# A weight stream through places in SBUF: norms in place, Z as a ring place, one single-use place more, and loads in another order

## The reference

```python
def first_block(x, ...):
    for layer in range(2):
        m = conv_mixer(x, ...) if layer % 2 == 0 else rglru_mixer(x, ...)
        x = layer_norm(ALPHA * x + m, ln1_g[layer], ln1_b[layer])
        f = moe(x, w_router, b_router, moe_w1[layer], moe_w3[layer], moe_w2[layer])
        x = layer_norm(ALPHA * x + f, ln2_g[layer], ln2_b[layer])
    return x

def moe(...):                      # 16 experts, the best 2 of one group of 4 for each token
    ...
    hb = jax.nn.silu(xb @ w1[e]) * (xb @ w3[e])      # w1, w3, w2: 1024 x 1024 each, fp32
    return hb @ w2[e]

def rglru_mixer(...):
    u = x @ w_in;  y, xr = split(u);  xr = causal_depthwise_conv(xr, c_dw) + c_dw_b
    r = sigmoid(heads(xr) @ w_gate_a + b_gate_a);  i = sigmoid(heads(xr) @ w_gate_x + b_gate_x)
    log_a = -8 * r * softplus(-lam);  a = exp(log_a)
    h = associative_scan(a, sqrt(1 - a * a) * (i * xr))     # h[t] = a[t] h[t-1] + b[t]
    return (gelu(y) * h) @ w_out
```

## Time and profile before

| | us |
|---|---|
| runs (3) | 1814.17, 1814.87, 1815.21 |
| median | 1814.87 |
| profiled execution, its own device time | 1813.63 |
| span of the profiled execution | 1812.1 |
| PE busy in the span | 1719.1 (95%) |
| DVE busy | 798.0 (44%) |
| ACT busy | 618.4 (34%) |
| the DMA queue q1 (SP's) | 541.10 MB, 74.5% of 16 engines' span |

### The profile page before, as it was taken

How to read it: one execution, slowest core, us unless ns; L and a number is a source line. 1 busy time by engine, 2 the same in 40 slices (tenths; PEclk the granted TensorE clock), 3 DMA queues, 4 the chain that set the end, 5 groups by cost and what they waited for, 6 DMA issues and landing times.

```text
span 1812.1 us, 23943 instructions
## 1 busy us (share of the span) xinstructions
PE 1719.1 (95%) x9988; PEld 1111.4 (61%) x9988; DVE 798.0 (44%) x1538; ACT 618.4 (34%) x1179; POOL 121.2 (7%) x143
## 2 busy tenths in 40 slices
...
GB/s 390 204 218 418 422 423 422 422 424 420 420 420 418 242 173 422 424 422 423 422 423 422 419 420 420 221 138 140 166 184 186 186 163 163 120 125 186 186 185 25
DMA packets 75810, 544.88 MB, mean 301 GB/s; under 512 B 8496, under 2 KB 8496, under 8 KB 10032
## 3 DMA queue, kind: packets, MB, share of 16 engines
q1 hardware_dynamic: 75024, 541.10, 74.5%
...
## 4 chain that ended last, share of the span: by engine, by line
PE 65%; DMA 23%; DVE 7%; ACT 3%; issue 1%; POOL 1%; SPq 1%; DVEq 0%; ACTq 0%
PE PS L1076 21%; DMA ring<-in_w 13%; PE PS L350 12%; PE PS L352 11%; PE PS L351 11%; DMA F<-in_w 6%; PE PS L1053 2%; DMA ring<-in_a_w_in 2%; PE PS L1088 2%; DVE wl L333 2%; DMA ring<-in_odd_w_in 2%; PE PS L789 1%; ACT wh L327 1%; PE PS L554 1%; SPq L315 1%
## 5 line engine op out<-in xcount | busy, mean ns | idle before, releaser
L1076 PE MATMUL PS<-ring,F 128*64 128x512 f32 x2112 | 477.0, 597 | 38.7 <-DMA ring<-in_w 33.6
L333 DVE TENSOR_TENSOR wl<-ring,wh 128x512 fp32r<-128x512 f32 x512 | 368.3, 738 | 170.3 <-ACT wh L327 167.8
L327 ACT ACTIVATE wh<-ring 128x512 fp32r<-128x512 f32 x512 | 319.5, 631 | 271.7 <-PE PS L352 266.0
L1076 PEld LDWEIGHTS PS<-ring,F 128*64 128x64 f32 x2112 | 143.6, 136 | 354.7 <-issue 258.7
L350 PE MATMUL PS<-xh,wl 128*128 128x256 f32 x1168 | 336.6, 288 | 2.4 <-DVE wl L333 2.3
L351 PE MATMUL PS<-xl,wh 128*128 128x256 f32 x1168 | 330.4, 283 | 0.0
L352 PE MATMUL PS<-xh,wh 128*128 128x256 f32 x1168 | 330.3, 283 | 0.0
L350 PEld LDWEIGHTS PS<-xh,wl 128*128 128x128 f32 x1168 | 223.8, 192 | 5.7 <-DVE wl L333 2.7
L351 PEld LDWEIGHTS PS<-xl,wh 128*128 128x128 f32 x1168 | 223.9, 192 | 0.6
L352 PEld LDWEIGHTS PS<-xh,wh 128*128 128x128 f32 x1168 | 223.9, 192 | 0.0
L350 PE MATMUL PS<-wh,xl 128*128 128x512 f32 x352 | 142.5, 405 | 6.9 <-DVE xl L467 3.4
...
## 6 DMA issues: line engine op xcount, KB each, us to landing
ring<-in_w SPq DMA_DIRECT2D x264, 1024.0 KB, 26.4
F<-in_w SPq DMA_DIRECT2D x60, 1024.0 KB, 26.2
ring<-in_ffn_up SPq DMA_DIRECT2D x44, 1024.0 KB, 4.9
early<-in_w SPq DMA_DIRECT2D x40, 1024.0 KB, 26.4
ring<-in_ffn_down SPq DMA_DIRECT2D x22, 1024.0 KB, 4.9
Z<-in_w SPq DMA_DIRECT2D x10, 1024.0 KB, 25.9
XT<-in_w SPq DMA_DIRECT2D x10, 1024.0 KB, 25.1
ring<-in_even_w_in SPq DMA_DIRECT2D x9, 1024.0 KB, 19.6
```

Source lines behind the costliest of these rows:

```text
L327: act.e.activation(self.wh[:, p % NPIECE, :], self.piece_source(p), ACT.Copy).then_inc(*self.up("w_hi", p))
L333: dve.e.tensor_tensor(self.wl[:, p % NPIECE, :], self.piece_source(p), f32(self.wh[:, p % NPIECE, :]), ALU.subtract).then_inc(*self.up("w_ ...
L1076: t = pe.e.matmul(PS[64 * half:64 * half + 64, bank, :], lhs(k), weights[:, a:a + 512], start=(k == 0), stop=(k == 7))
```

## The change

- **Norms behind mixers in place.** `vector_residual` writes ALPHA * x + m back to X; the norm and the transposes then work on X. Behind `moe0` the norm goes from PSUM to X as well, behind `moe1` it still goes to Z. The new function `norm_buffer` says which. The code for overflowing experts keeps its saved values in F in place of Z (it isn't executed with these inputs).
- **Z a ring place.** Up to `aq0` Z is a thirteenth ring place, for dense chunks too.
- **One single place more.** Slot 23 is F[2304:4352]. Only the fourth chunk of a MoE (w1 of expert 0, last quarter) uses it, and LOAD_ORDER moves that chunk's load back, from fourth to eighteenth of its MoE. So 24 chunks can be in SBUF when a MoE begins, in place of 23.
- **Loads in the order in which places come free.** FIRST_SLOTS has a new order. In layer 0 eleven ring loads come ahead of the F places. In layer 1 the F places 16, 15, 14 and 13 stand between ring loads, each for itself.
- **The recurrences' buffers by head.** xc, Tt, ig and R of one head lie together (2048 columns), which is slot 16 for head 0, 15 for head 1, 14 for head 2 and 13 for head 3; each of these waits only for its head's `od_join`. The buffers gq and odd_gh, odd_gl move to F[12672:14720].
- **The two row DMAs** leave ACT. SP issues them behind the third `aq0` chunk (`sync_rows`).

```diff
-RING, SMALL_RING, EXTRA = 12, 7, 11
+RING, SMALL_RING, EXTRA = 12, 7, 12
...
-F_SLOTS, SPLIT_SLOTS, Z_SLOT, XT_SLOT = range(12, 17), range(17, 21), 21, 22
-FIRST_SLOTS = ([12, 13] + [None] * 8 + [14, 15, 16] + [None] * 4 + [17, 18, 19, 20, 21, 22],
-               [None] * 8 + [12, 13, 14, 15, 16] + [None] * 4 + [17, 18, 19, 20, 21, 22])
+F_SLOTS, SPLIT_SLOTS, Z_SLOT, XT_SLOT, ONCE_SLOT = range(12, 17), range(17, 21), 21, 22, 23
+FIRST_SLOTS = ([12, 13] + [None] * 11 + [14, 15, 16, None, ONCE_SLOT, None, 17, 18, 19, 20, XT_SLOT],
+               [None] * 8 + [16, 15, None, None, 14, None, 13, None, 12, ONCE_SLOT, None, 17, 18, 19, 20, XT_SLOT])
+LOAD_ORDER = list(range(len(KIND)))
 
 
 def _place_stream():
+    for layer in range(2):
+        m, at = CHUNK[f"moe{layer}"], FIRST_SLOTS[layer].index(ONCE_SLOT)
+        LOAD_ORDER[m + 3:m + at + 1] = LOAD_ORDER[m + 4:m + at + 1] + [m + 3]
     last, loads = [None] * (RING + EXTRA), [0] * (RING + EXTRA)
-    for n, kind in enumerate(KIND):
-        slots = list(range(RING if n < CHUNK["aq0"] else SMALL_RING))
+    SLOT.extend([None] * len(KIND))
+    PREVIOUS.extend([None] * len(KIND))
+    LOADS.extend([None] * len(KIND))
+    for position, n in enumerate(LOAD_ORDER):
+        slots = [*range(RING), Z_SLOT] if n < CHUNK["aq0"] else list(range(SMALL_RING))
         slot = None
-        if kind == "expert":
+        if KIND[n] == "expert":
             layer = int(n >= CHUNK["moe1"])
-            i = n - CHUNK[f"moe{layer}"]
-            if i < RING + EXTRA:
+            i = position - CHUNK[f"moe{layer}"]
+            if i < len(FIRST_SLOTS[layer]):
                 slot = FIRST_SLOTS[layer][i]
             elif i < 128:
-                slots += range(RING, RING + EXTRA)
+                slots += [*F_SLOTS, *SPLIT_SLOTS, XT_SLOT]
         if slot is None:
             slot = min(slots, key=lambda x: -1 if last[x] is None else last[x])
-        SLOT.append(slot)
-        PREVIOUS.append(last[slot])
+        SLOT[n], PREVIOUS[n] = slot, last[slot]
         last[slot] = n
         loads[slot] += n > 0
-        LOADS.append(loads[slot])
+        LOADS[n] = loads[slot]
 
...
-                                  for n, a in (("odd_gh", 13312), ("odd_gl", 13824))]
+                                  for n, a in (("odd_gh", 13696), ("odd_gl", 14208))]
...
-            self.Z[:, :, :].rearrange("p h d -> p (h d)"), self.XT[:, :, :].rearrange("p k t -> p (k t)")]
+            self.Z[:, :, :].rearrange("p h d -> p (h d)"), self.XT[:, :, :].rearrange("p k t -> p (k t)"),
+            self.F[:, 2304:4352]]
...
-        slot, mixer, norm = SLOT[n], ("ow_out" if layer else "ew_out"), ("ln2" if layer else "ln0")
-        if n - CHUNK[f"moe{layer}"] >= RING + EXTRA:
+        slot, mixer = SLOT[n], ("ow_out" if layer else "ew_out")
+        if slot == Z_SLOT or n - CHUNK[f"moe{layer}"] >= len(FIRST_SLOTS[layer]):
             return []
-        if slot in F_SLOTS:
-            return [] if layer == 0 and slot < 14 else [self.at("g_lo", mixer, 3), self.at("w_used", PIECES[mixer] + 3)]
+        if layer == 0 and slot in (12, 13):
+            return []
+        if layer and slot in range(13, 17):
+            return [self.at("od_join", 16 - slot)]
+        if slot in F_SLOTS or slot == ONCE_SLOT:
+            return [self.at("g_lo", mixer, 3), self.at("w_used", PIECES[mixer] + 3)]
         if slot in SPLIT_SLOTS:
             return [self.at("w_used", PIECES[mixer] + 15)]
-        return [self.at("turned", norm, 3) if slot == Z_SLOT else self.at("tokens_turned", layer, 3)]
+        return [self.at("tokens_turned", layer, 3)]
 
     def sync_load(self, first, last):
         sp = self.sp
-        for n in range(first, min(last, len(KIND))):
+        for n in LOAD_ORDER[first:last]:
+            if n == CHUNK["aq0"] + 3:
+                self.sync_rows()
             if KIND[n] == "expert" and SLOT[n] >= RING:
                 sp.wait_ge(*self.extra_free(n))
             if PREVIOUS[n] is not None:
                 sp.wait_ge(self.released(PREVIOUS[n]))
             src = self.source(n)
             sp.e.dma_start(self.chunk(n)[:, 0:src.shape[-1]], src).then_inc(self.ring_sems[SLOT[n]], 16)
+
+    def sync_rows(self):
+
+        self.sp.wait_ge(self.at("expert_chunk", CHUNK["moe1"] + 131))
+        for r in range(2):
+            self.sp.e.dma_start(self.F[:, 9472 + r * 1024:10496 + r * 1024], self.A["rows"][r, :].partition_broadcast(128)
+                                ).then_inc(self.s_row, 16)
...
-        return self.Z[:, h, d * 512:d * 512 + 512], self.at("resid", stage, h, d)
+        return self.X[:, h, d * 512:d * 512 + 512], self.at("resid", stage, h, d)
+
+    def norm_buffer(self, stage):
+
+        return self.Z if stage == "moe1" else self.X
...
-            self.vector_residual("ew_out", p, 8, m, ALPHA, self.Z, *self.x_in, stats=True)
+            self.vector_residual("ew_out", p, 8, m, ALPHA, self.X, *self.x_in, stats=True)
...
-                act.wait_ge(at("xg0", 1, 7), at("xg1", 1, 7))
-                for r in range(2):
-                    act.e.dma_start(self.F[:, 9472 + r * 1024:10496 + r * 1024], self.A["rows"][r, :].partition_broadcast(128)
-                                    ).then_inc(self.s_row, 16)
...
-        y, xc, Tt, ig, R = (self.fv(a, 8) for a in (2048, 4096, 6144, 8192, 10240))
-        gq = [self.F[:, 12288 + i * 512:12800 + i * 512].rearrange("p (k t) -> p k t", k=2) for i in range(2)]
+
+
+        y = self.fv(2048, 8)
+        by_head = self.F[:, 4480:12672].rearrange("p (h n j t) -> p n h j t", h=4, n=4, j=2)
+        xc, Tt, ig, R = (by_head[:, n] for n in range(4))
+        gq = [self.F[:, 12672 + i * 512:13184 + i * 512].rearrange("p (k t) -> p k t", k=2) for i in range(2)]
...
-            s = slice(4 * i, 4 * i + 4)
+            s = slice(2 * i, 2 * i + 2)
             act.wait_ge(at("od_rate", i))
-            act.e.activation(R[:, s, :], Tt[:, s, :], ACT.Exp, scale=-2.0).then_inc(*up("od_decay", i))
+            act.e.activation(R[:, s], Tt[:, s], ACT.Exp, scale=-2.0).then_inc(*up("od_decay", i))
             act.wait_ge(at("od_decay", i))
-            act.e.activation(Tt[:, s, :], Tt[:, s, :], ACT.Tanh).then_inc(*up("od_rate_tanh", i))
+            act.e.activation(Tt[:, s], Tt[:, s], ACT.Tanh).then_inc(*up("od_rate_tanh", i))
...
-        for c in (2 * h, 2 * h + 1):
-            t = dve.e.tensor_tensor_scan(ig[:, c, :], R[:, c, :], xc[:, c, :], 0.0, ALU.mult, ALU.add)
+        for j in range(2):
+            t = dve.e.tensor_tensor_scan(ig[:, h, j, :], R[:, h, j, :], xc[:, h, j, :], 0.0, ALU.mult, ALU.add)
...
-            self.vector_residual("ow_out", p, 8, m, ALPHA, self.Z, at("x_tokens", "od", 3), stats=True)
+            self.vector_residual("ow_out", p, 8, m, ALPHA, self.X, at("x_tokens", "od", 3), stats=True)
...
-            loaded = after + (SMALL_RING if layer else RING)
+            loaded = after + (SMALL_RING if layer else RING + 1)
```

More of the change, by code:

```diff
@@ L1395, in moe_overflow @@
     def moe_overflow(self, layer, flag):
-        nc = self.nc
+        nc, saved = self.nc, self.overflow_views()["saved"]
         with nc.If(flag > 0):
@@ L1630, in odd_scalar @@
                 for k in (2 * c, 2 * c + 1):
-                    t = act.e.activation(xc[:, k, :], self.bank2(c)[:, k % 2, :], ACT.Identity, scale=cw[:, k, 3:4],
+                    t = act.e.activation(xc[:, c, k % 2, :], self.bank2(c)[:, k % 2, :], ACT.Identity, scale=cw[:, k, 3:4],
                                          bias=cb[:, k:k + 1])
@@ L1644, in gate @@
             for c in (2 * h, 2 * h + 1):
-                t = act.e.activation((Tt, ig)[g][:, c, :], self.bank2(4 * g + h)[:, c % 2, :], ACT.Tanh, scale=0.5,
+                t = act.e.activation((Tt, ig)[g][:, h, c % 2, :], self.bank2(4 * g + h)[:, c % 2, :], ACT.Tanh, scale=0.5,
                                      bias=hb[:, 8 * g + c:8 * g + c + 1])
```

39 lines of the change are left out of this document (19 added, 20 removed).

## The result

| | before | after |
|---|---|---|
| runs | 1814.17, 1814.24, 1814.87, 1815.21 | 1800.89, 1801.40, 1801.89, 1802.62 |
| median, us | 1814.55 | 1801.64 |
| span of the profiled execution | 1812.1 | 1799.6 |
| q1, MB and share of 16 engines' span | 541.10, 74.5% | 542.15, 75.5% |
| PE busy in the span | 1719.1 (95%) | 1715.4 (95%) |

The ratio is 0.9929 [0.9912, 0.9946], 12.9 us less; 1800.9 us were forecast. q1 carries 1.05 MB more because the two row DMAs are now issued by SP.

The account below looks back on a forecast made before the run. The DMA stream was taken to bound the experts, idle ahead of both MoEs while loads wait for places. Terms 2.3 + 9.2 + 2.5 = 14.0 us off 1813.63 give 1799.6, plus 1.24 for the median: 1800.9 us, range 1797.5 to 1806.5.

Parts of the forecast that it names:

- dips: DMA share falls just before 141.7 and about 692.5 us, the sign that all places were full.
- the chain turning one and two experts later: Chain of waits turns from PE to DMA one expert later in moe0, two in moe1.
- rows with no wait: DVE at L2080, which reads the rows, does not wait for their later DMAs; 3.6 us to spare.
- the two ring loads: First mixer: SP issues two ring loads between 90 and 105 us, after ew_out splits ending at 92.6 and 104.0 us.
- B: Rival: the rows' 2.5 us come back as DVE at L2080 or first aq0 splits wait; 1803.4 us, 7%.
- C: Rival: a join holds SP until the mixer's end, loads bunch up as before; 7.5 us gained, 1807.4 us, 5%.
- D: Rival: PE becomes the bound of the experts, no gain; 1814.9 us, 4%.
- E: Rival: slower, loads moved into the mixers slow their engines through shared SBUF; 1818.9 us, 4%.
- moe0's end earlier: First mixer: expert 0's fifth-chunk load lands at 156.3 us, not 159.7; 2.3 us taken, 1.9 to 3.4.
- restart in moe1: Second mixer: the load for the fifth chunk's place lands at 709.4 us, not 719.7; 9.2 us taken, 9.1 to 10.3.
- row DMAs: moe1's end: 1 MB of rows, moved behind the third aq0 chunk, no longer stands ahead; gain 2.5 us.
- added work: Mixers: residuals to X 0.06 us, six ACT calls over gapped blocks at worst 1.8 us; nothing taken.

Follow-up runs that it names:

- e8_after_again: The changed kernel run again with no edit, on the same chip; median 1800.10 us over 6 runs, ratio 0.9931 [0.9918, 0.9944].
- e1: The changed kernel with the two row DMAs issued by ACT in expert 15 again; median 1804.25 us, ratio 0.9948 [0.9935, 0.9962].
- e2: The changed kernel with the row DMAs on SP's queue, but eight expert chunks ahead of moe1's end; median 1804.05 us, ratio 0.9945 [0.9931, 0.9959].

## Why the prediction was right, step by step

The time was right to 0.8 us, the saving less so: 14.0 us were forecast, and it is 12.9 by the medians and 12.5 by the spans. The mechanism held at the signs that were named: idle stretches used, dips, two early restarts, the chain turning one and two experts later, rows with no wait. One sign was off: the first of the two ring loads goes out at 89.3 us, not behind 90. The forecast took both from the wrong splits. They wait for splits that end at 89.25 and 99.14 us in the changed kernel, not for those that ended at 92.6 and 104.0 before; as both lie well ahead of 111 us, this cost nothing. The rivals fall: B (no wait at L2105), C (four F loads from 638.50 to 663.43 us), D (PE is not the end: the chain consists of DMAs from 379.75 and 930.71 us), E (the second mixer is 0.2 us shorter, the start 0.2 us).

Its terms against the runs:

| term | forecast | measured |
|---|---|---|
| moe0's end earlier | 2.3 (1.9 to 3.4) | 1.4 (571.85 - 570.42); 1.9 in e8_after_again; by bytes 1.3 |
| restart in moe1 | 9.2 (9.1 to 10.3) | 10.6 or 10.9, less the rows' 3: 7.6 to 7.9; by bytes 8.5 |
| row DMAs | 2.5 | 2.8 to 3.3 (e1, e2); what the bytes leave: 2.2 |
| added work | 0 (0 to 1.8) | 0: mixers 0.2 us shorter each |
| sum | 14.0 | 12.5 (spans) |

**Which step was mis-sized.** Both restart terms were taken from the landing of one load, issue plus 4.8 us, against its landing before. The two loads did land 3.2 and 11.4 us earlier (5.2 and 5.3 us after their issue; 1.6 of the 11.4 us is moe0's shift, 703.0 in place of 704.6 us), yet the MoEs end 1.4 and, with the rows' share of 3 and moe0's shift of 1.4 taken off 12.2, 7.8 us earlier. The step that fails is "the lead of this load is the lead of the stream". The very next load shows it: issued at 153.1 us, it lands at 160.9 us, where it was 162.2. Of the 3.2 us 1.3 are left.

The forecast also said that from the fifth chunk's load on PE releases faster than the stream fills and the queue is full. Windows behind that load in moe0 and in moe1, the kernel before and then the changed one:

```profile
153.00:159.00 6.00, 4.96 (x28) 2.06 (x26) 1.02 (x2) 0.87 (x2) 0.00 (x0) 1.00 0.98 392
704.00:711.00 7.00, 6.21 (x32) 2.19 (x29) 1.31 (x3) 0.00 (x0) 0.00 (x0) 1.00 1.01 421
```

```profile
153.00:159.00 6.00, 4.96 (x28) 1.91 (x24) 1.02 (x2) 1.07 (x2) 0.00 (x0) 1.00 0.91 320
704.00:711.00 7.00, 5.96 (x32) 2.35 (x30) 1.02 (x2) 1.09 (x2) 0.00 (x0) 1.00 0.97 343
```

The queue isn't full yet: (392 - 320) x 6 us = 0.43 MB and (421 - 343) x 7 us = 0.55 MB, 1.0 and 1.3 us of pace, that the forecast did not take off. Bytes tell the lead better than landings. What q1 had moved from 0 to 170, to 720 and to 1090 us (packets, MB, share of the engines' time), before and then changed:

```profile
q1 hardware_dynamic: 7167, 50.17, 73.0%
...
q1 hardware_dynamic: 36275, 262.13, 88.3%
...
q1 hardware_dynamic: 57672, 417.96, 92.6%
```

```profile
q1 hardware_dynamic: 7243, 50.73, 75.2%
...
q1 hardware_dynamic: 36843, 266.30, 90.4%
...
q1 hardware_dynamic: 58252, 422.17, 94.0%
```

The lead is 0.56 MB at 170 us, 1.3 us of pace at 421 GB/s, and 4.17 MB at 720 us. At 590 us, ahead of the second restart, it was 0.61 MB (227.46 and 226.85 MB), so this restart brings 3.56 MB, 8.5 us. Both lie under the bound that I had called the least (1.9 and 9.1). A load lands when the last of its packets has, and in a full queue the last trails the mean pace, which 159.7 against 158.2 us had already shown; that this is the rest of the difference is likely, but not shown. From 720 us on the lead stays: 4.21 MB at 1090 us, 10.0 us. moe1 ends 12.2 us earlier, and the 2.2 us between are close to the rows' 2.5, which no longer stand ahead of its last chunks. In e8_after_again it is 4.42 MB, 10.5 us, and an end 13.0 us earlier, which leaves 2.5.

**The time to landing.** At the restarts the two loads took 5.2 and 5.3 us to land. The Trainium skill, "DMA: Bandwidth & Descriptors", section "Bandwidth", has 6.15 us for 1 MB on the GpSimd path; by it the sum would have been 11.3 us, and 12.5 was measured. The trace does not agree with that figure of the Trainium skill for SP's queue, and the measurement decides. That 11.3 would have come out a little closer than 14.0 is not the merit of that figure: the loads landed when the row said, within 0.5 us, and the miss lay in what their landing is worth.

**What was luck.** That the time came out within 0.8 us. The two restarts were 0.9 and 1.4 us under their terms; the rows at 3 us in place of 2.5 and the slightly shorter mixers gave some of it back, and the median of the kernel before, from which the forecast starts, came out 0.3 us lower with a fourth run (1814.55 for 1814.87). The profiled executions of before and after also both ran at the full clock up to 1790 us and fell below it only at the very end (0.999 in the mean). A median over more runs moves by a microsecond or two with the number of executions that have a stretch at the lower clock (1800.10 and 1801.64 for one kernel).
